# A two-layer hybrid trunk on one core: Toeplitz tiles in partition groups, score matmuls side by side, stick-breaking attention by pairs of heads

## The chip, the core and the metric

One NeuronCore of a Trainium2 chip runs the whole kernel. The metric is the device time of one execution in microseconds (us); the kernel before has 1127.8 as the median of three runs (1125.94 to 1127.84). One further execution was profiled.

## What is computed

Two layers over 256 tokens of width 1024, all in fp32. The parts that the change touches, cut from the reference:

```python
# stick-breaking attention: 8 heads of 64, strictly causal
z = einsum('bhqd,bhkd->bhqk', q, k) * 64 ** -0.5
log_1mb = where(mask, log_sigmoid(-z), 0)
later = cumsum(log_1mb, axis=3, reverse=True) - log_1mb
w = where(mask, exp(log_sigmoid(z) + later), 0);  y = w @ v
# differential attention: 4 heads, two 64-wide score components each
p1 = softmax(mask(q1 @ k1.T)); p2 = softmax(mask(q2 @ k2.T)); o = (p1 - lam * p2) @ v
# S5 state-space branch: 32 groups of 16 channels, 64 complex states
x_t = lam_bar * x_(t-1) + b_bar @ u_t;  y_t = Re(c @ x_t) + d * u_t
```

Around these stand RMSNorms, one wide input projection, gated merging, cross-attention and a squared-ReLU MLP, all as large matrix products.

## The kernel before

**Units.** A layer's weights are walked in units (`plan`), two chunks of 128x1024 each, by SyncE's DMA into a ring `raw`. ScalarE (ACT, `fn`, L897) rounds a chunk to fp32r, the rounded format, as `w_hi`; VectorE (DVE, `tt`, L1311) makes the remainder `w_lo` (`prep`, two units ahead, L917 and L1316); TensorE (PE) does three products hi*hi, hi*lo, lo*hi (`three`, L1788). "T" units have 256-column matmuls (48) or "N" units 512-column ones (24). Units 0 to 13 are u, sq, sk, sv, dq, dk, dv (two each), 14 to 25 the gates, 26 and 27 glu; up and down units of the MLP come last.

**Sides.** `side_stages` (L127) hangs small stages behind units, sorted by `RANK` (L232) for units 7 to 26. PE runs a unit, then its side. VectorE's loop (L1723) is: evacuate the unit's banks, `stage` of each side stage, `prep`, then `later` of each. ScalarE's (L1190) is the same with `prep` ahead of the stages up to unit 15. Each engine keeps its order; semaphores count bank fills (`full`) and releases (`free`), and `before` makes a matmul wait for the last user of its bank. There are eight PSUM banks: A0 to A3, T0, T1 (units), X0, X1 (stages).

**Stick-breaking**, head h: behind unit 6+h `sb_s` (L1972) puts scores into X0 as 256 and 128 columns (the causal triangle, keys on the partitions), VectorE masks them into z (L1606), then in `later` ScalarE takes |z|, exp, ln (L1157) and VectorE adds max(z, 0) (L1684) to give nl = -log(1-beta). Behind unit 7+h `sb_u` (L1983) multiplies nl by a triangle `tri` and by `ones` into X1, in fp32, to get the cumulative sums; VectorE subtracts, ScalarE exponentiates. Behind 8+h `sb_p` (L1992) multiplies with the values into 64 partitions of A3; after two heads the bank is split into hi and lo. z and nl are double-buffered.

**Differential**, j = 0 to 7 (two query tiles by four heads): behind 16+j `da_s` (L2006) makes two components into X0 and X1, 128 columns (j < 4) or 256; behind 17+j `da_t` (L2015) transposes the weights into X1, copied out by ScalarE (L1113); behind 18+j `da_p` multiplies by the values. `RANK` puts da_t ahead of the next da_s.

**Toeplitz tables.** `p_k` (L1902) makes for each of 16 pairs of groups a 32x128 tile (4 fp32 matmuls of 32 stationary columns, L1911, and a 32x32 diagonal, L1913), four tiles to a bank, n = 0 to 3; ScalarE copies them into `kt` (L997), 4 copies for each n, shifted to 4 places. Layer 0's set lies behind units 5 and 6 in A0 and A1, layer 1's behind two down units of layer 0's MLP in X0 and X1. Next come `p_bt` transposes in the same banks, copied by ScalarE. Four `ssm_in` stages stand behind units 9 to 12 (VectorE in `later`, L1449, signal `s_ready`) and four `ssm_out` behind 11 to 14. ScalarE's evacuation of dv (unit 13) waits for all four `s_ready` (L1037).

GpSimd builds constants and the tables of powers and phases.

## Time and profile before

| | us |
|---|---|
| median of three runs | 1127.8 |
| the profiled execution, its own time | 1125.67 |
| its span | 1124.0 |
| PE busy | 1075.9 (96%) |
| DVE busy | 738.7 (66%) |
| ACT busy | 581.3 (52%) |
| POOL (GpSimd) busy | 170.2 (15%) |

Busy is the time in which at least one instruction of the engine ran, as a share of the span. A fp32 matmul stands as two rows, one for each pass; its end is modelled, so neighbouring matmuls overlap in the rows, and the time from start to start is the better measure. Shapes are written rows*columns of the stationary side, then output partitions x columns.

### The profile page before, as it was taken

To read this page: it belongs to the slowest core of one execution; us is meant where nothing else is said; L and a number is where in the kernel's file an instruction comes from. 1 tells how busy PE (TensorE), PEld (TensorE's weight loads), DVE (VectorE), ACT (ScalarE), POOL (GpSimd) and SP (SyncE) were. 2 spreads that over 40 slices of the span, in tenths; PEclk is the share of its full clock that TensorE was granted. 3 is DMA by queue.
4 is the path that set the end of the run, shared out by engine and by line. 5 is a ranking of instruction groups with operands and counts; after the bars stand their busy time and mean duration, and the time that the engine had idled before them with its cause. 6 is when DMAs were issued, how large, how long until landed. Compare 5 with 4: busy or idle time off the path is not lost. (4 is left out here: it accounts for less than half of the span.)

```text
span 1124.0 us, 18664 instructions
## 1 busy us (share of the span) xinstructions
PE 1075.9 (96%) x7186; PEld 967.0 (86%) x7186; DVE 738.7 (66%) x1071; ACT 581.3 (52%) x907; POOL 170.2 (15%) x305
## 2 busy tenths in 40 slices
PE   4989999999999899999989999999999999999996
PEld 4967889989998799987979878998998979989995
DVE  5864965778876565795465468477787647555554
ACT  7445445546665555544654444544555556444442
POOL 5992100000000003996000001000000000000000
PEclk9999999999999999999999999999999999999998
DMA  8723235446554296553556532364465535666662
GB/s 226 209 73 113 89 100 155 147 142 209 175 166 139 88 255 189 178 179 107 161 183 189 167 108 90 95 193 138 151 223 156 161 117 169 187 188 188 188 187 76
DMA packets 148988, 175.62 MB, mean 156 GB/s; under 512 B 26658, under 2 KB 106660, under 8 KB 148900
## 3 DMA queue, kind: packets, MB, share of 16 engines
q1 hardware_dynamic: 148484, 174.16, 51.4%
q8 instruction: 58, 0.95, 0.3%
q10 hardware_dynamic: 416, 0.26, 0.2%
q14 instruction: 30, 0.25, 0.1%
HBM read 171.25 MB, written 3.15 MB: 155 GB/s over the span
## 5 line engine op out<-in xcount | busy, mean ns | idle before, releaser
L1311 DVE TENSOR_TENSOR s_w_lo<-s_raw,s_w_hi 128x1024 fp32r<-128x1024 f32 x312 | 377.5, 1239 | 138.9 <-ACT s_w_hi L897 135.4
L897 ACT ACTIVATE s_w_hi<-s_raw 128x1024 fp32r<-128x1024 f32 x312 | 321.4, 1055 | 202.4 <-PE p_T L1791 137.6
L1789 PE MATMUL p_T<-s_hT_hi,s_w_hi 128*128 128x256 f32 x1152 | 330.6, 287 | 7.5 <-DVE s_hT_lo L1380 5.8
L1790 PE MATMUL p_T<-s_hT_lo,s_w_hi 128*128 128x256 f32 x1152 | 326.8, 284 | 0.0
L1791 PE MATMUL p_T<-s_hT_hi,s_w_lo 128*128 128x256 f32 x1152 | 326.7, 284 | 0.0
L1789 PEld LDWEIGHTS p_T<-s_hT_hi,s_w_hi 128*128 128x128 f32 x1152 | 221.8, 192 | 12.8 <-issue 11.4
L1790 PEld LDWEIGHTS p_T<-s_hT_lo,s_w_hi 128*128 128x128 f32 x1152 | 222.0, 193 | 0.4
L1791 PEld LDWEIGHTS p_T<-s_hT_hi,s_w_lo 128*128 128x128 f32 x1152 | 221.8, 193 | 0.0
L1789 PE MATMUL p_A<-s_w_hi,s_bT_hi 128*128 128x512 f32 x320 | 125.3, 392 | 2.4 <-DVE s_bT_lo L1311 2.4
L1790 PE MATMUL p_A<-s_w_lo,s_bT_hi 128*128 128x512 f32 x320 | 124.7, 390 | 0.0
L1791 PE MATMUL p_A<-s_w_hi,s_bT_lo 128*128 128x512 f32 x320 | 124.6, 389 | 0.0
L1789 PEld LDWEIGHTS p_A<-s_w_hi,s_bT_hi 128*128 128x128 f32 x320 | 60.2, 188 | 15.1 <-issue 3.2
L1791 PEld LDWEIGHTS p_A<-s_w_hi,s_bT_lo 128*128 128x128 f32 x320 | 60.1, 188 | 12.7
L1790 PEld LDWEIGHTS p_A<-s_w_lo,s_bT_hi 128*128 128x128 f32 x320 | 60.1, 188 | 11.7
L725 POOL TENSOR_TENSOR s_small<-s_small 128x16 f32<-128x16 f32 (+1 forms) x130 | 55.8, 453 | 7.0 <-ACT s_small L897 4.7
L1789 PE MATMUL p_T<-s_w_hi,s_hT_hi 128*128 128x512 f32 x128 | 51.9, 406 | 2.4 <-issue 2.4
L897 ACT ACTIVATE s_att<-s_att 128x384 f32<-128x384 f32 (+1 forms) x68 | 36.1, 532 | 32.8 <-DVE s_att L1311 31.0
L1790 PE MATMUL p_T<-s_w_lo,s_hT_hi 128*128 128x512 f32 x128 | 50.6, 396 | 0.0
L1791 PE MATMUL p_T<-s_w_hi,s_hT_lo 128*128 128x512 f32 x128 | 50.6, 396 | 0.0
L897 ACT ACTIVATE s_bT_hi<-s_att 128x512 fp32r<-128x512 f32 x32 | 20.2, 632 | 57.8 <-DVE s_att L1311 57.8
L725 POOL TENSOR_TENSOR s_small<-s_col,s_small 128x16 f32<-128x16 f32 x4 | 1.0, 263 | 310.5 <-ACT s_small L897 310.5
L1789 PE MATMUL p_T<-s_bT_hi,s_w_hi 128*128 128x256 f32 x160 | 45.9, 287 | 0.3 <-issue 0.3
(270 smaller groups left out, 1688.5 us busy)
## 6 DMA issues: line engine op xcount, KB each, us to landing
s_raw<-in_w_in SPq DMA_DIRECT2D x104, 512.0 KB, 3.6
s_raw<-in_w_up SPq DMA_DIRECT2D x64, 512.0 KB, 3.7
s_raw<-in_w_down SPq DMA_DIRECT2D x64, 512.0 KB, 3.8
s_raw<-in_w_branch SPq DMA_DIRECT2D x24, 512.0 KB, 3.9
s_raw<-in_w_out SPq DMA_DIRECT2D x16, 512.0 KB, 4.6
s_raw<-in_w_xkv SPq DMA_DIRECT2D x16, 512.0 KB, 3.7
s_raw<-in_ssm_w_glu SPq DMA_DIRECT2D x8, 512.0 KB, 3.8
s_raw<-in_w_xq SPq DMA_DIRECT2D x8, 512.0 KB, 3.7
```

What stands on the lines that cost most here:

```text
L725: return nc.gpsimd.tensor_tensor(o, i0, i1, op)
L897: return nc.scalar.activation(o, i, f, **kw)
L1311: return V.tensor_tensor(o, i0, i1, op)
L1789: mm(o, lhi, rhi, start=first, stop=False, **kw)
L1790: mm(o, lhi, rlo, start=False, stop=False, **kw)
L1791: return mm(o, llo, rhi, start=False, stop=last, **kw)
```

## The change

The Toeplitz tiles of a table all go into one bank in the first p_k stage: tile 4n+q lies in partitions 32q to 32q+31, columns from 128n, and the four q of a step are issued one after the other; the second p_k stage only copies. Layer 0's table keeps A0, layer 1's X0. Stick-breaking runs by pairs p = 0 to 3: sb_s behind unit 6+2p with the heads' scores in X0 and X1, sb_u behind 7+2p, sb_p behind 8+2p; z and nl hold both heads and have one buffer. nl is split into nl_hi (ScalarE) and nl_lo (VectorE), both fp32r, and the cumulative sums are two fp32r passes of each, with `tri` and `ones` stored as fp32r (built in `att` by GpSimd and copied at the start by VectorE). da_s waits for both banks before its first matmul, and da_t goes to A1.

```diff
-    for h in range(SB_HEADS):
-        after(6 + h, "sb_s", h)
-        after(7 + h, "sb_u", h)
-        after(8 + h, "sb_p", h)
+    for p in range(SB_PAIRS):
+        after(6 + 2 * p, "sb_s", p)
+        after(7 + 2 * p, "sb_u", p)
+        after(8 + 2 * p, "sb_p", p)
...
-        "p_ct": ["X0", "X1"], "sb_s": ["X0"], "sb_u": ["X1"], "turn": ["X0", "X1"],
-        "da_s": ["X0", "X1"], "da_t": ["X1"], "da_o": ["X1"],
+        "p_ct": ["X0", "X1"], "sb_s": ["X0", "X1"], "sb_u": ["X0", "X1"], "sb_p": ["A3"], "turn": ["X0", "X1"],
+        "da_s": ["X0", "X1"], "da_t": ["A1"], "da_o": ["X1"],
...
-        [[["A0", "A1"], ["X0", "X1"]][s[1]][s[2] % 2]] if s[0] in ("p_k", "p_bt") else
+        [[["A0", "A1"], ["X0", "X1"]][s[1]][s[2] % 2]] if s[0] == "p_bt" or s[0] == "p_k" and s[2] == 0 else
...
-        ["A3"] if s[0] == "sb_p" and s[1] % 2 == 0 else
...
+        at = -(-nc.sbuf_base // 32) * 32
...
+        att_r = nc.alloc_sbuf_tensor_at("s_att_r", [P, 2560], F32R, offset=at)
...
-        tri = sb("tri", [P, P])
-        ones = sb("ones", [P, P])
+        tri_r, ones_r = sb("tri", [P, P], F32R), sb("ones", [P, P], F32R)
+        ones = ones_r[:, :].bitcast(F32)
+        tri_0, ones_0 = att[:, 1024:1152], att[:, 1152:1280]
...
-        z_b = [att[:, 768 * i:768 * i + 384] for i in range(2)]
-        nl_b = [att[:, 768 * i + 384:768 * i + 768] for i in range(2)]
+        z, nl = (att[:, 768 * i:768 * i + 768].rearrange("p (h n) -> p h n", h=2) for i in (0, 1))
+        nl_lo, nl_hi = (att_r[:, 768 * i:768 * i + 768].rearrange("p (h n) -> p h n", h=2) for i in (1, 2))
...
-                    b = stage_banks(s)[0]
-                    act.wait_ge(*st.at(*full_at(l, b, s)))
+                    use = ("p_k", t, 0)
+                    b = stage_banks(use)[0]
+                    act.wait_ge(*st.at(*full_at(l, b, use)))
...
-                    for j in range(BL):
-                        rows = slice(32 * j, 32 * j + 32)
-                        ins = fn(kt[rows, 4 * n:4 * n + 4, 32 * j:P], src[0:32, :, 0:P - 32 * j])
-                        ins.then_inc(*st.sig(*freed(l, b, s))) if j == BL - 1 else ins.then_inc(*st.mid())
+                    every = kt[:, :, :].rearrange("p (i q) c -> p q i c", q=4)
+                    for q in (2 * n, 2 * n + 1):
+                        for j in range(BL):
+                            rows = slice(32 * j, 32 * j + 32)
+                            ins = fn(every[rows, q, :, 32 * j:P], src[32 * q:32 * q + 32, :, 0:P - 32 * j])
+                            last = n and q == 3 and j == BL - 1
+                            ins.then_inc(*st.sig(*freed(l, b, use))) if last else ins.then_inc(*st.mid())
...
                     elif kind == "sb_u":
-                        z = z_b[s[1] % 2]
+                        act.wait_ge(*st.at(*freed(l, "X0", s)))
...
-                    elif kind == "sb_p" and s[1] % 2:
+                    elif kind == "sb_p":
...
-                        fn(bT_hi[:, 4 + s[1] // 2, :], bank["A3"][:, 0:T]).then_inc(*st.sig(sb_hi))
+                        fn(bT_hi[:, 4 + s[1], :], bank["A3"][:, 0:T]).then_inc(*st.sig(sb_hi))
...
-                        act.wait_ge(*st.at(*full_at(l, "X1", s)))
+                        act.wait_ge(*st.at(*full_at(l, "A1", s)))
...
-                        fn(pT_b[j % 2][:, 0:nk], bank["X1"][:, 0:nk]).then_inc(*st.sig(*freed(l, "X1", s)))
+                        fn(pT_b[j % 2][:, 0:nk], bank["A1"][:, 0:nk]).then_inc(*st.sig(*freed(l, "A1", s)))
...
-                        z, nl = z_b[s[1] % 2], nl_b[s[1] % 2]
...
+                        act.wait_ge(*st.at(*freed(l, "X1", s)))
                         fn(nl, z, ACT.Abs).then_inc(*st.mid())
...
+                        act.wait_ge(*st.at(nl_made, s[1] + 1))
+                        fn(nl_hi, nl).then_inc(*st.sig(nl_split))
...
+            V.tensor_copy(tri_r[:, :], tri_0).then_inc(*pst.mid())
+            V.tensor_copy(ones_r[:, :], ones_0).then_inc(*pst.mid())
...
-                        h = s[1]
-                        if h >= 2:
-                            dve.wait_ge(*st.at(sbp_done, h - 1))
-                        dve.wait_ge(*st.at(*full_at(l, "X0", s)))
-                        z = z_b[h % 2]
-                        tt(z[:, 0:T], bank["X0"][:, 0:T], mask_s, ALU.min).then_inc(*st.mid())
-                        tt(z[:, T:384], bank["X0"][:, T:384], mask_s[:, 0:P], ALU.min)\
-                            .then_inc(*st.sig(*freed(l, "X0", s)))
+                        p = s[1]
+                        if p:
+                            dve.wait_ge(*st.at(sbp_done, p))
+                        for h, b in enumerate(("X0", "X1")):
+                            dve.wait_ge(*st.at(*full_at(l, b, s)))
+                            tt(z[:, h, 0:T], bank[b][:, 0:T], mask_s, ALU.min).then_inc(*st.mid())
+                            tt(z[:, h, T:384], bank[b][:, T:384], mask_s[:, 0:P], ALU.min)\
+                                .then_inc(*st.sig(*freed(l, b, s)))
...
-                        z = z_b[s[1] % 2]
-                        dve.wait_ge(*st.at(*full_at(l, "X1", s)))
-                        tt(z, z, bank["X1"][:, 0:384], ALU.subtract).then_inc(*st.sig(*freed(l, "X1", s)))
-                    elif kind == "sb_p" and s[1] % 2:
-                        k = s[1] // 2
-                        dve.wait_ge(*st.at(sb_hi, k + 1))
-                        tt(bT_lo[:, 4 + k, :], bank["A3"][:, 0:T], f32(bT_hi[:, 4 + k, :]), ALU.subtract)\
-                            .then_inc(*st.sig(*freed(l, "A3", ("sb_p", s[1] - 1))))
+                        for h, b in enumerate(("X0", "X1")):
+                            dve.wait_ge(*st.at(*full_at(l, b, s)))
+                            tt(z[:, h, :], z[:, h, :], bank[b][:, 0:384], ALU.subtract)\
+                                .then_inc(*st.sig(*freed(l, b, s)))
+                    elif kind == "sb_p":
+                        p = s[1]
+                        dve.wait_ge(*st.at(sb_hi, p + 1))
+                        tt(bT_lo[:, 4 + p, :], bank["A3"][:, 0:T], f32(bT_hi[:, 4 + p, :]), ALU.subtract)\
+                            .then_inc(*st.sig(*freed(l, "A3", s)))
...
-                            dve.wait_ge(*st.at(*full_at(l, "X1", ("da_t", j - 2))))
+                            dve.wait_ge(*st.at(*full_at(l, "A1", ("da_t", j - 2))))
...
-                        z, nl = z_b[s[1] % 2], nl_b[s[1] % 2]
...
-                         .then_inc(*st.sig(nl_ready))
+                         .then_inc(*st.sig(nl_made))
+                        dve.wait_ge(*st.at(nl_split, s[1] + 1))
+                        tt(nl_lo, nl, f32(nl_hi), ALU.subtract).then_inc(*st.sig(nl_ready))
...
-                    elif kind == "p_k":
-                        t, n = s[1:]
+                    elif kind == "p_k" and s[2] == 0:
+                        t, c = s[1], 2 * GC
...
-                        for q in range(4):
-                            i, c = 4 * n + q, 2 * GC
+                        for n in range(4):
...
-                                mm(bank[b][0:c, q * P:q * P + P], bN0[:, r, i, :], ct[:, r, i, :],
-                                   start=(r == 0), stop=False, skip_group_check=True)
-                            ins = mm(bank[b][0:c, q * P:q * P + c], ident[0:c, 0:c], diag_d[:, i, :],
-                                     start=False, stop=True, skip_group_check=True)
+                                for q in range(4):
+                                    mm(bank[b][c * q:c * q + c, n * P:n * P + P], bN0[:, r, 4 * n + q, :],
+                                       ct[:, r, 4 * n + q, :], start=(r == 0), stop=False, skip_group_check=True)
+                            for q in range(4):
+                                ins = mm(bank[b][c * q:c * q + c, n * P:n * P + c], ident[0:c, 0:c],
+                                         diag_d[:, 4 * n + q, :], start=False, stop=True, skip_group_check=True)
...
-                        h = s[1]
-                        r, c = slice(HD * (h % 2), HD * (h % 2) + HD), h // 2
-                        if h == 0:
+                        c = s[1]
+                        if c == 0:
...
-                        mm(bank["X0"][:, 0:T], qk[r, 4 + c, 0:P], qk[r, c, :], start=True, stop=True)
-                        mm(bank["X0"][:, T:T + P], qk[r, 4 + c, P:T], qk[r, c, P:T], start=True, stop=True)\
-                            .then_inc(*st.sig(full["X0"]))
+                        pe.wait_ge(*st.at(*before(l, "X1", s)))
+                        heads = [(b, slice(HD * h, HD * h + HD)) for h, b in enumerate(("X0", "X1"))]
+                        for b, r in heads:
+                            mm(bank[b][:, 0:T], qk[r, 4 + c, 0:P], qk[r, c, :], start=True, stop=True)
+                        for b, r in heads:
+                            mm(bank[b][:, T:T + P], qk[r, 4 + c, P:T], qk[r, c, P:T], start=True, stop=True)\
+                                .then_inc(*st.sig(full[b]))
                     elif kind == "sb_u":
-                        nl = nl_b[s[1] % 2]
                         pe.wait_ge(*st.at(nl_ready, s[1] + 1))
-                        pe.wait_ge(*st.at(*before(l, "X1", s)))
...
-                        o = bank["X1"]
-                        mm(o[:, 0:384], tri[:, :], nl, start=True, stop=True)
-                        mm(o[:, P:T], ones[:, :], nl[:, T:384], start=False, stop=True, skip_group_check=True)\
-                            .then_inc(*st.sig(full["X1"]))
+                        for h, b in enumerate(("X0", "X1")):
+                            pe.wait_ge(*st.at(*before(l, b, s)))
+                            o = bank[b]
+                            mm(o[:, 0:384], tri_r[:, :], nl_hi[:, h, :], start=True, stop=False)
+                            mm(o[:, 0:384], tri_r[:, :], nl_lo[:, h, :], start=False, stop=True)
+                            mm(o[:, P:T], ones_r[:, :], nl_hi[:, h, T:384], start=False, stop=False, skip_group_check=True)
+                            mm(o[:, P:T], ones_r[:, :], nl_lo[:, h, T:384], start=False, stop=True, skip_group_check=True)\
+                                .then_inc(*st.sig(full[b]))
                     elif kind == "sb_p":
-                        h = s[1]
-                        w = z_b[h % 2]
-                        pe.wait_ge(*st.at(w_ready, h + 1))
-                        if h == 0:
+                        p = s[1]
+                        pe.wait_ge(*st.at(w_ready, p + 1))
+                        if p == 0:
...
-                        if h % 2 == 0:
-                            pe.wait_ge(*st.at(*before(l, "A3", s)))
-                        r = slice(HD * (h % 2), HD * (h % 2) + HD)
-                        c = slice(HD * h, HD * h + HD)
-                        mm(bank["A3"][r, 0:T], vN[:, 0, c], w[:, 0:T], start=True, stop=True, skip_group_check=True)
-                        mm(bank["A3"][r, P:T], vN[:, 1, c], w[:, T:384], start=False, stop=True, skip_group_check=True)\
-                            .then_inc(*st.sig(sbp_done))
+                        pe.wait_ge(*st.at(*before(l, "A3", s)))
+                        heads = [(h, slice(HD * h, HD * h + HD), slice(HD * (2 * p + h), HD * (2 * p + h) + HD))
+                                 for h in range(2)]
+                        for h, r, c in heads:
+                            mm(bank["A3"][r, 0:T], vN[:, 0, c], z[:, h, 0:T], start=True, stop=True, skip_group_check=True)
+                        for h, r, c in heads:
+                            ins = mm(bank["A3"][r, P:T], vN[:, 1, c], z[:, h, T:384], start=False, stop=True,
+                                     skip_group_check=True)
+                        ins.then_inc(*st.sig(sbp_done))
                     elif kind == "da_s":
...
+                        pe.wait_ge(*st.at(*before(l, "X0", s)))
+                        pe.wait_ge(*st.at(*before(l, "X1", s)))
...
-                            pe.wait_ge(*st.at(*before(l, b, s)))
...
-                        pe.wait_ge(*st.at(*before(l, "X1", s)))
+                        pe.wait_ge(*st.at(*before(l, "A1", s)))
...
-                            ins = turn(bank["X1"][:, kb * P:kb * P + P], p_b[j % 2][:, 0, kb * P:kb * P + P])
-                        ins.then_inc(*st.sig(full["X1"]))
+                            ins = turn(bank["A1"][:, kb * P:kb * P + P], p_b[j % 2][:, 0, kb * P:kb * P + P])
+                        ins.then_inc(*st.sig(full["A1"]))
...
-                        pe.wait_ge(*st.at(*freed(l, "X1", ("da_t", s[1]))))
+                        pe.wait_ge(*st.at(*freed(l, "A1", ("da_t", s[1]))))
```

Left out are the constants SB_PAIRS = 4, the memsets of tri and ones, signal sizes, ScalarE's bank name for da_t, and waits that name the last p_k or sb_p stage.

## Rows read from the trace of the kernel before

**Rows 1.** The page's head and part 1.
```profile
span 1124.0 us, 18664 instructions
...
PE 1075.9 (96%) x7186; PEld 967.0 (86%) x7186; DVE 738.7 (66%) x1071; ACT 581.3 (52%) x907; POOL 170.2 (15%) x305
```

**Rows 2.** Groups by line; out<-in xcount | busy, mean ns | idle before.
```profile
L1790 PE MATMUL p_T<-s_hT_lo,s_w_hi 128*128 128x256 f32 x1152 | 326.8, 284 | 0.0
...
L1790 PE MATMUL p_A<-s_w_lo,s_bT_hi 128*128 128x512 f32 x320 | 124.7, 390 | 0.0
```

**Rows 3.** Timeline of PE behind unit 9, layer 0: start, us, engine, line.
```profile
107.53 0.65 PE L2003 MATMUL p_A<-s_att,s_vN 128*64 128x256 f32 x2
...
108.33 0.91 PE L1989 MATMUL p_X<-s_att,s_tri 128*128 128x384 f32 x2
...
109.39 0.70 PE L1980 MATMUL p_X<-s_qk 64*128 64x256 f32 x2
...
110.24 2.00 PE L1947 MATMUL p_A<-s_uB,s_bt 128*128 128x63 f32 x16
```

**Rows 4.** Timeline of PE, first two Toeplitz tiles, layer 0.
```profile
57.22 0.62 PE L1911 MATMUL p_A<-s_ct,s_tmp 128*32 128x128 f32 x4
57.77 0.24 PE L1913 MATMUL p_A<-s_att,s_ident 32*32 32x32 f32 x2
57.94 0.62 PE L1911 MATMUL p_A<-s_ct,s_tmp 128*32 128x128 f32 x4
```

**Rows 5.** Timeline of PE, three of the differential score stages, layer 0.
```profile
184.34 0.49 PE L2013 MATMUL p_X<-s_qk 64*128 64x128 f32 x4
...
198.00 1.00 PE L2013 MATMUL p_X<-s_qk 64*128 64x128 f32 x4
...
220.07 1.38 PE L2013 MATMUL p_X<-s_qk 64*128 64x256 f32 x4
```

**Rows 6.** Timeline of VectorE and ScalarE behind unit 6, layer 1.
```profile
633.05 0.62 DVE L1311 TENSOR_TENSOR s_att<-p_X,s_masks 128x256 f32<-128x256 f32 x2 [4.49 <-PE p_X L1981]
...
633.59 2.35 DVE L1311 TENSOR_TENSOR s_w_lo<-s_raw,s_w_hi 128x1024 fp32r<-128x1024 f32 x2
...
633.79 1.64 ACT L897 ACTIVATE s_att<-s_att 128x384 f32<-128x384 f32 x3 [0.54 <-DVE s_att L1311]
...
635.97 0.56 DVE L1684 SCALAR_TENSOR_TENSOR s_att<-s_att 128x384 f32<-128x384 f32 x1
```

**Rows 7.** Groups by line: ScalarE on 1024 columns, VectorE on 768.
```profile
L897 ACT ACTIVATE s_w_hi<-s_raw 128x1024 fp32r<-128x1024 f32 x312 | 321.4, 1055 | 202.4 <-PE p_T L1791 137.6 <-PE p_A L1791 57.9 <-DMA s_raw<-in_w_down 1.7
...
L1311 DVE TENSOR_TENSOR s_qk<-s_vN,s_small 128x768 f32<-128x768 f32 x4 | 3.7, 962 | 0.2
```

**Rows 8.** Timeline around unit 6, layer 0.
```profile
63.92 0.69 DVE L1512 SCALAR_TENSOR_TENSOR s_qk<-p_T,s_r_row 128x512 f32<-128x512 f32 x1
...
64.71 0.55 PE L1789 MATMUL p_T<-s_w_hi,s_hT_hi 128*128 128x512 f32 x1 [1.60 <-issue]
...
75.04 1.77 ACT L897 ACTIVATE s_kt<-p_A 32x512 f32<-32x512 f32 x4 [1.85 <-PE p_A L1913]
```

**Rows 9.** Busy us by stretch; after POOL the granted clock of PE.
```profile
64.96:68.37 3.41, 3.41 (x9) 2.65 (x9) 3.38 (x3) 0.02 (x1) 3.33 (x4) 0.50 0.00 0
81.28:92.66 11.38, 9.75 (x49) 7.46 (x49) 9.06 (x10) 6.74 (x11) 8.22 (x7) 1.00 0.32 94
112.04:122.20 10.16, 10.16 (x54) 8.03 (x54) 9.59 (x18) 4.22 (x6) 0.00 (x0) 1.00 0.32 103
147.88:158.94 11.06, 11.06 (x63) 8.93 (x62) 6.73 (x14) 3.95 (x6) 0.00 (x0) 1.00 0.32 96
```

**Rows 10.** Timeline of VectorE and ScalarE, first state stage and dv, layer 0.
```profile
116.32 0.65 DVE L1311 TENSOR_TENSOR s_gates<-p_A,s_phase 128x504 f32<-128x504 f32 x1
...
121.86 0.56 DVE L1311 TENSOR_TENSOR s_att<-s_att,p_X 128x384 f32<-128x384 f32 x1
...
153.72 1.26 ACT L897 ACTIVATE s_dv<-p_T,s_stat 128x512 f32<-128x512 f32 x2 [7.33 <-PE p_T L1791]
```

26 lines of the change are left out of this document (13 added, 13 removed).

## The prediction

> **What bounds the kernel now.** I read the page first: TensorE (PE) is busy for 96% of the span [rows 1], so time leaves the kernel only where PE work goes away and nothing else takes its place. Next the groups by line: the weight matmuls, which the change leaves alone, differ by 106 ns between 256 and 512 columns, 0.41 ns a column [rows 2]. The small fp32 matmuls cost more per column, and the timeline shows by how much. At the end of a unit one stick-breaking head takes PE from 107.53 to 110.24: weighted values 0.80 us, cumulative sums 1.06, scores of the next head 0.85 [rows 3]. Each fp32 matmul is there as two passes (x2). The Toeplitz tile starts every 0.72 us (57.22, 57.94), of which four 128-column passes and their drain take 0.55 [rows 4]. The differential scores show what lets two matmuls run together: at 184.34 two heads' halves, rows 0 to 63 and 64 to 127 into two banks, are busy for 0.49 us with four passes of 128 columns. At 198.00 the same four take 1.00 (1.38 with 256 columns at 220.07), since the second half waited for the copy out of X1 [rows 5].
>
> **Toeplitz tables, second set** (layer 1's, made in layer 0's MLP). Before: 16 tiles of 0.725 = 11.6 us [rows 4]. After: 4 rounds. In a round four tiles hold four column groups, each with 4 passes. If they overlap as the row groups of [rows 5] do, a round is one tile's passes and drain, 0.55, the small diagonal pair, 0.17, and some stagger, 0.05: 0.77, in all 3.1 us. Saved 8.5. If they don't, the 64 passes stay (0.11 each, 7.0 us) and only 12 of 16 changes of tile shape go: some 8.5 us in all, saved 3.1. I take the first: the rows nearest to it, though they are row groups, show four passes in the time of two. ACT's 16 copies keep their sizes, and PE is waited on by nobody there, so all of it counts.
> Against it, the Trainium skill, TensorE: Matmul & The Clock Gate, Part 3: Packing small matmuls, states that a weight load overlaps a running matmul only when its row group differs; these share their rows. By that rule this term would be 3.1 us, and rival A is the case. The Trainium skill's page TensorEngine Tiling (Array Packing), Key Properties, has tiles load and multiply in parallel; no row here decides between them.
>
> **Toeplitz tables, first set** (layer 0, units 5 and 6): the same 8.5 us on PE, but I book nothing. (a) The first half ended at 62.9 and PE then waited until 64.71 for VectorE's evacuation at 63.92 [rows 8], which doesn't move. (b) Now all tiles lie before unit 6, and p_bt's first bank A0 is free only after ScalarE's last 8 copies. They stand behind the w_hi that waits for unit 6 and ends at 73.19 (75.04 less the idle 1.85), and 8 copies are 2 x 1.77 [rows 8]: 76.7. PE, free at 72.0, waits 4.7. Unit 7 starts at about 78.3, not 81.28 [rows 9]. (c) Then comes the new chain of pair 0, worked out next: 78.2 + 6.9, and some 2.5 to 3 more because GpSimd slows VectorE there (9.06 us busy in unit 7 [rows 9] for what takes 7.3 elsewhere, and twice the columns now): about 88. With both sums, VectorE's two subtractions, the exponential and two bank copies unit 8 starts near 92.7. Before it was 92.66 [rows 9]. Net 0.
>
> **Stick-breaking by pairs.** Before, two heads: 2 x 2.71 = 5.42 us [rows 3]. After: scores of two heads in two row groups 0.86; values in two column groups 0.82 (1.45 without overlap); sums, per head two passes of 384 columns and two of 128. 384 by the line of [rows 2] is 0.17. For 128 columns in the rounded format there is no row: from below 0.06 by the same line, from above 0.22, the cost of the fp32 pair. I take 0.115, near one fp32 pass of 128 columns (four and a drain are 0.55 [rows 4]), because each needs its own weight load. Sums: 2 x (0.34 + 0.23) = 1.14. A pair is 2.82: saved 2.6, over 8 pairs 20.8 us.
>
> **What is added, and who waits.** The chain from scores to sums gets twice as wide and two steps longer. For 384 columns it was: VectorE's minimum 0.62, ScalarE's three functions 1.64, VectorE's 0.56 [rows 6]. For 768: minima 1.25; three functions of 0.85 (1024 columns take 1.055 [rows 7]), 2.6; the add 0.99; then new ScalarE's rounding 0.85 and VectorE's remainder 0.96 [rows 7]; with hand-overs 6.9 us from the last score. PE has one unit, 5.65 us (10.16 from unit to unit [rows 9], less a side of 4.51, 107.53 to 112.04, [rows 3, 9]), and what stands behind the scores in their side. So in layer 1 PE waits at the sums 1.2 us in unit 7 and 0.95 in unit 9; in layer 0 1.0 in unit 9, and in unit 7, where GpSimd's table work slows VectorE, over 2. While ScalarE stands on the add, its evacuation and next w_hi stand behind it; each has a unit to spare.
> From unit 9 to 13 VectorE is the second bound: 9.59 of 10.16 us of a unit [rows 9]. A state-space stage takes it 5.5 us (116.32 to 121.86 [rows 10]; there are four), the weights 2.35 a unit [rows 6]. Its work per pair grows by 0.75 and it stands about 1.2 for ScalarE's rounding. The first state stage starts 4 us earlier (no scores in unit 9), and the four then take 3.6 longer: they end near 152.9. ScalarE's evacuation of dv waits for exactly that in the code; before, it began at 153.72 [rows 10]. Unit 14 needs its first bank, 0.7 later. So unit 14 starts near 153.7 in place of 158.94 [rows 9], though PE could be there 1.4 earlier. Units 14 and 15 give 0.9 each.
> Layer 0, from unit 8: nominal 9.4, less 1.0 and 1.4: 7.0. Layer 1: nominal 10.4, less 1.2, 0.95 and 1.6 for dv: 6.6.
>
> **Differential scores.** Both waits now stand ahead, and the transposed weights go to A1, so X0 and X1 are free when PE comes. The first of eight was paired already; three of 128 columns go from 1.00 to 0.49 and four of 256 from 1.38 to 0.70 (two more passes' worth, 0.21) [rows 5]: 4.2 a layer, 8.4. The last of a layer waited longest, but VectorE is late there and takes that back.
>
> **Edits at nothing.** Two 128-column roundings at the start stand where VectorE waits for positions to land; GpSimd's memsets only change their target; DMAs are the same.
>
> **Sum.** 8.5 + 0 + 7.0 + 6.6 + 8.4 = 30.5 us. The profiled execution took 1125.7 us by its own time (span 1124.0 [rows 1]) and would become 1095.2. It was 2.1 below the median of 1127.8, which becomes **1097**.
>
> **Rivals.**
> A, column groups don't overlap. For: no row shows it, and the four tiles share their rows. Against: row groups do it at once. Tables lose 5.4, values 0.64 a pair where PE is the bound (unit 14 in layer 0 hides most): 1.2 and 2.5. 1097 + 9 = 1106.
> B, the waits at the sums are longer. For: the chain is as long as a unit, and ScalarE may be in an evacuation or w_hi (2.0 us) when the minima come. 2 us more at six of eight pairs, partly absorbed by dv: 1106 to 1109. It needs no fault in the matmul terms.
> C, slower than before: each wait of PE now lets the clock fall. The one fall in the trace followed short Toeplitz work and a 1.6 us wait, and left a granted clock of 0.50 for 3.4 us [rows 9], worth 1.5 us. Its place is the sums' waits: if each of the eight grows by 3 us and brings a fall, 8 x 4.5 = 36 us stand against 30.5, and it ends at 1133. It decides from 30.5 / 8 = 3.8 us a pair. Against: one unit's weights, 5.65 us of dense work, stand between any two waits, and two falls in a row have no row.
> D, better: nl is ready in time, dv doesn't bind: 5 us less, 1092.
> E, the pairs don't overlap even in rows (another order of issue): the scores were in this order once and did. 1104 with overlap elsewhere.
> The first set's wait of 4.7 may bring a fall of its own (+1.5), and the old one may go (-1.5); both are in the range. If 128 columns cost the fp32 price, 8 x 0.42, +3.
>
> **How the numbers follow.** Forecast 0.50, A 0.24, B 0.11, D 0.10, E 0.03, C 0.02. The likeliest is 1097; its own width is 1092 to 1101. The range, 1089 to 1110, takes in A, most of B and D. A measurement of this kernel tells about 0.2% (2.3 us) from no change; every case but C is faster by more. Faster 0.96, same 0.02, slower 0.02.
>
> **What would show it.** Right: Toeplitz rows with starts a few ns apart by fours and some 3 us per table; values of two heads in 0.8 us; a PE gap of about 1 us ahead of the sums in units 7 and 9, ended by VectorE's remainder; unit 8 of layer 0 near 92.7; dv evacuated near 153; differential scores busy for at most 0.7 us. Wrong: 109 ns steps through the Toeplitz rounds (A), gaps over 2 us at the sums (B), granted clock at 1.2 GHz in several stretches (C), a first table that pays on its own.

## The result, and the profile after

The changed kernel takes **1109.7 us** (median of four, 1108.89 to 1111.68) against 1127.8 for the kernel before in the same job: ratio 0.9846, interval 0.9828 to 0.9863. The forecast was 1097. 18 us were gained and not 30.5.

The page's head, part 1 and the clock line of part 2 of the changed kernel; a digit of PEclk stands for 1/40 of the span:

```profile
span 1108.6 us, 18576 instructions
...
PE 1039.0 (94%) x7186; PEld 949.3 (86%) x7186; DVE 745.5 (67%) x1073; ACT 581.8 (52%) x883; POOL 176.7 (16%) x305
...
PEclk9989999999999999999999999999999999999998
```

Against [rows 1], PE is busy for 36.9 us less, and the span is only 15.4 shorter. TensorE's work did go away; some 21 us of it turned into idle time. PE was busy for 96% and is for 94%.

**The matmuls are as forecast.** Timeline of PE and its weight loads (PEld) of the changed kernel: the first two Toeplitz rounds, a pair's values and next scores, and one of the last differential scores.

```profile
57.56 0.38 PEld L1925 LDWEIGHTS p_A<-s_ct,s_tmp 128*32 128x32 f32 x16
57.56 0.64 PE L1925 MATMUL p_A<-s_ct,s_tmp 128*32 128x128 f32 x16
58.13 0.26 PE L1928 MATMUL p_A<-s_att,s_ident 32*32 32x32 f32 x8
58.33 0.64 PE L1925 MATMUL p_A<-s_ct,s_tmp 128*32 128x128 f32 x16
...
100.51 0.65 PE L2019 MATMUL p_A<-s_att,s_vN 128*64 128x256 f32 x4
...
101.31 0.70 PE L1995 MATMUL p_X<-s_qk 64*128 64x256 f32 x4
...
216.83 0.70 PE L2032 MATMUL p_X<-s_qk 64*128 64x256 f32 x4
```

Sixteen passes of four column groups are busy for 0.64 us, where four passes of one took 0.62 in [rows 4]; a round is 0.77 (57.56 to 58.33), as forecast. The values of two heads take 0.80 us for 0.82, their scores 0.86 for 0.86, and differential scores of 256 columns 0.70 where they took 1.38 in [rows 5].

**Where the rest went** is read from stretches between points that both kernels have. The view gives, for each stretch, its length, busy time of PE, PEld, DVE, ACT and POOL, the granted clock as a share of 2.4 GHz, and DMA. The kernel before, from 60 us to unit 8 of layer 0, on to the transposes ahead of the differential part, to the start of layer 1 (which takes in the second table set), to its unit 0 and on to its transposes:

```profile
60.00:92.66 32.66, 28.00 (x159) 20.47 (x159) 21.17 (x21) 16.85 (x31) 28.56 (x40) 0.95 0.23 69
92.66:176.76 84.10, 84.10 (x503) 70.08 (x501) 53.00 (x87) 38.39 (x58) 6.25 (x12) 1.00 0.32 95
176.76:585.36 408.60, 400.96 (x2743) 364.83 (x2742) 279.85 (x388) 224.76 (x355) 84.20 (x130) 1.00 0.55 167
585.36:625.28 39.92, 36.54 (x303) 35.92 (x301) 23.14 (x34) 20.19 (x33) 0.00 (x0) 1.00 0.65 180
625.28:723.55 98.27, 97.44 (x555) 80.29 (x553) 62.67 (x99) 44.59 (x65) 6.23 (x12) 1.00 0.37 110
```

The same stretches of the changed kernel:

```profile
60.00:94.90 34.90, 22.86 (x113) 18.19 (x108) 23.08 (x23) 18.93 (x32) 30.20 (x40) 0.80 0.21 67
94.90:175.12 80.22, 76.29 (x499) 66.61 (x497) 54.68 (x85) 35.85 (x45) 8.43 (x12) 0.98 0.31 99
175.12:574.68 399.56, 388.50 (x2744) 357.27 (x2742) 279.48 (x388) 225.26 (x355) 84.39 (x130) 1.00 0.55 171
574.68:615.18 40.50, 37.54 (x302) 37.23 (x301) 23.32 (x34) 20.42 (x33) 0.00 (x0) 0.96 0.61 178
615.18:710.68 95.50, 89.24 (x555) 76.63 (x553) 66.23 (x100) 44.09 (x53) 8.78 (x12) 0.98 0.36 113
```

Layer 0 from unit 8 gains 3.9 us (84.10 to 80.22; forecast 7.0), the third stretch 9.0 (forecast 4.2 + 8.5), layer 1's last 2.8 (forecast 6.6). Up to unit 8 2.2 are lost where none was expected. Two things are new: PE idles in stretches where it had been busy throughout, and its clock is lower.

**The new waits**, in the view of what PE waited for (in all, times, longest):

```profile
PE p_X L2004 <- DVE s_att_r L1323: 6.4, 5, 1.9
...
PE p_T L1803 <- issue: 5.5, 4, 4.4
PE p_A L1787 <- ACT s_kt L900: 4.9, 1, 4.9
PE p_T L1803 <- ACT s_dv L900: 4.7, 2, 2.4
PE p_A L1787 <- DVE s_att L1710: 3.5, 2, 1.7
```

They are: the sums, for VectorE's remainder; unit 6 ("issue", 4.4, against 1.6 in [rows 8]; VectorE's evacuation for it starts at 64.26, behind table work); p_bt of the first set, for ScalarE's copies; unit 14, for dv; the last differential transposes of each layer, for the weights.

**The clock.** The stretches at half clock (1.2 GHz), in the same columns as above:

```profile
65.36:68.77 3.41, 3.41 (x10) 2.64 (x9) 3.38 (x4) 0.00 (x0) 3.33 (x3) 0.50 0.00 0
75.60:82.42 6.82, 5.12 (x20) 4.13 (x21) 1.47 (x5) 2.88 (x7) 6.51 (x14) 0.50 0.01 2
89.25:92.66 3.41, 3.41 (x15) 3.41 (x16) 1.39 (x3) 2.33 (x4) 2.13 (x3) 0.50 0.26 100
157.52:160.93 3.41, 3.28 (x15) 3.28 (x16) 2.13 (x3) 3.38 (x5) 0.00 (x0) 0.50 0.00 0
577.36:580.77 3.41, 2.86 (x14) 2.89 (x15) 2.97 (x8) 2.53 (x8) 0.00 (x0) 0.50 0.00 0
693.41:696.82 3.41, 3.41 (x18) 3.41 (x18) 2.13 (x3) 3.00 (x4) 0.00 (x0) 0.50 0.00 0
```

Below such a stretch is called a fall. Before there was one (the first of [rows 9]); in either kernel one more begins behind the last matmul and costs none. Each of the six comes during or just behind a wait, but most waits bring none: from 60 us on, 24 steps from one matmul to the next are longer than 1.1 us. Summed over the matmuls in the falls, the steps from start to start are 9.9 us longer than the same steps elsewhere (1.6 before). This is called the excess: what half clock costs if all of it lies on the path.

So there are three accounts of the missing 15 us: the waits alone (rival W below), the waits and the clock behind them (theory G), and matmuls dearer than they look. They need experiments.

### The profile page after: what moved, and what is told of

It is laid out like the page before. It is cut to its first block and busy times, and to the rows that moved or that the text cites. A ratio compares the mean times of both kernels' runs of the same rounds, so it can differ in the third digit from the quotient of the medians.

```text
span 1108.6 us, 18576 instructions
## 1 busy us (share of the span) xinstructions
PE 1039.0 (94%) x7186; PEld 949.3 (86%) x7186; DVE 745.5 (67%) x1073; ACT 581.8 (52%) x883; POOL 176.7 (16%) x305
## 5 line engine op out<-in xcount | busy, mean ns | idle before, releaser
L1803 PEld LDWEIGHTS p_T<-s_hT_hi,s_w_hi 128*128 128x128 f32 x1152 | 223.6, 194 | 17.8 <-issue 11.4
L900 ACT ACTIVATE s_att<-s_att 128x768 f32<-128x768 f32 (+1 forms) x36 | 29.6, 823 | 30.1 <-DVE s_att L1323 29.0
```

The lines of the kernel that those rows point to most:

```text
L900: return nc.scalar.activation(o, i, f, **kw)
L1803: mm(o, lhi, rhi, start=first, stop=False, **kw)
```

## Experiments

Each run was timed in five rounds beside the kernel before on the same chip (medians 1126.2 to 1127.7).

### The parts one by one

**tables_only**: the kernel before, with p_k and its copies as in the change.

> The kernel before with the grouped Toeplitz rounds alone (both table sets), sums and differential scores as before. Theory G (the matmul terms of the prediction were right in size, and part of the gain is given back in new waits of TensorE and in granted-clock falls): the second set gives about 6.6 us (8.5 less a 2.2 us wait for ScalarE's copies), the first set 0 to 1 us (it ends early, waits about 5 us for the copies and runs 6.8 us at half clock): 1127.8 - 7 = about 1121. Rival S (the matmul terms themselves are smaller than forecast, the waits cost nothing): the rounds would take longer than 0.77 us each and the first set would still give something; about 1121 too, but with rounds of over 1 us. Rival F (the forecast's own term): 1119.3.

Measured 1124.0 (1121.0 to 1125.8), ratio 0.9971 (0.9960 to 0.9981): 2.5 us. The rounds take 0.77 us. The long waits stand where the changed kernel has them (4.9 us at unit 6, 5.3 at p_bt), and the profiled run has 10.4 us of excess. Nine runs of one program spread over 4.8 us, with mean clocks of 0.983 to 0.989 that do not sort them. The theory's waits and falls are both there, but it missed by 3 us of time, and by 4.5 of the 7 us of gain that it expected.

**diff_only**: the kernel before, with this alone (left out is the bank's name in the waits and copies of da_t):

```diff
-        "da_s": ["X0", "X1"], "da_t": ["X1"], "da_o": ["X1"],
+        "da_s": ["X0", "X1"], "da_t": ["A1"], "da_o": ["X1"],
...
+                        pe.wait_ge(*st.at(*before(l, "X0", s)))
+                        pe.wait_ge(*st.at(*before(l, "X1", s)))
                         for c, b in enumerate(("X0", "X1")):
-                            pe.wait_ge(*st.at(*before(l, b, s)))
```

> The kernel before with the change of the differential scores alone (both waits ahead, transposed weights into A1). Theory G: each layer gives 4.2 us on the scores and loses about 2 us in a wait ahead of the last transposes, so 2.5 us a layer, 1122.8. Rival F (the forecast's term, with no new wait): 1119.4. Rival I (the 2 us wait of the full change comes from the late stick-breaking work and not from this part): near 1119.4 as well, and no step over 1.5 us ahead of the last transposes.

Measured 1120.3 (1119.8 to 1120.6), ratio 0.9941 (0.9929 to 0.9953): 6.2 us, about 3 a layer, where G had 2.5 a layer. The 2 us step ahead of the last transposes is there in both layers (at 239.41 and 783.12), so I falls: the wait belongs to this part.

**pairs_only**: the kernel before, with the stick-breaking part alone.

> The kernel before with the stick-breaking part of the change alone (pairs of heads, sums in two passes of the rounded format); Toeplitz tiles and differential scores as before. The three parts measured apart: tables alone gave 2.5 us (1126.4 to 1124.0) and differential scores alone 6.2. If they add up, this part is worth 16.7 - 2.5 - 6.2 = 8.0 us against the 20.8 less waits of 5.7 that the prediction booked: 1118.4. Theory G has it between 1117 and 1120, with waits over 1 us ahead of the sums of both first pairs of a layer and 2.6 us ahead of unit 14. Rival X (the parts get in each other's way: the tables' early end brings the wait into unit 7): 1114 or less.

Measured **1127.7** (1120.5 to 1130.2), ratio 0.9995 (0.9976 to 1.0014). A part that takes 20 us of work from TensorE gives no time. Theory G had 1117 to 1120, and missed. Its first wait at the sums is the longest of all, and its falls are long. Timeline of the first sums of layer 0 of this kernel, and windows over four of its falls; the third line is the part of the second fall from the start of unit 14 on:

```profile
91.24 0.69 PE L1999 MATMUL p_X<-s_att_r,s_tri 128*128 128x384 f32 x1 [3.59 <-DVE s_att_r L1318]
```

```profile
90.09:96.92 6.83, 5.08 (x21) 4.71 (x22) 4.43 (x5) 5.19 (x8) 0.25 (x2) 0.50 0.09 36
158.36:165.19 6.83, 5.57 (x26) 5.57 (x27) 3.71 (x5) 4.00 (x5) 0.00 (x0) 0.50 0.00 0
159.62:165.19 5.57, 5.57 (x26) 5.57 (x27) 2.65 (x3) 3.26 (x4) 0.00 (x0) 0.50 0.00 0
...
660.12:666.95 6.83, 6.83 (x24) 5.91 (x23) 6.56 (x11) 1.18 (x2) 3.45 (x4) 0.50 0.01 3
707.90:714.73 6.83, 5.82 (x27) 5.82 (x28) 3.46 (x5) 4.21 (x6) 0.00 (x0) 0.50 0.00 0
```

The excess is some 16 us, over 10 of it in these four. The twelve runs fall into groups by their mean clock: 1120.5 to 1122.4 at 0.990 to 0.992, 1127.7 to 1128.1 at 0.981 to 0.983, 1129.7 to 1130.2 at 0.977 and 0.978. One program, up to 10 us apart, and the clock goes with it. The parts sum to 2.5 + 6.2 - 1.5 = 7 us against 18 together. By the fastest run of each (5.4, 6.7 and 5.7) they sum to 17.8. That would fit parts that add apart from the clock, but the fastest of up to twelve runs is a chosen one, and no run here shows it.

### Is the clock a cause?

**pairs_filled**: pairs_only with idle PE time filled by matmuls of the identity into a free bank.

```diff
+                def fill(b, use, n):
+                    pe.wait_ge(*st.at(*before(l, b, use)))
+                    for _ in range(n):
+                        mm(bank[b][:, 0:P], ident[:, :], ident[:, :], start=True, stop=True, skip_group_check=True)
...
+                    if kind == "sb_u":
+                        fill("X0", s, [14, 4, 0, 0][s[1]] if l == 0 else [5, 7, 0, 0][s[1]])
...
+                    if u == 14:
+                        fill("A3", ("sb_p", 3), 10)
```

> The kernel with the stick-breaking part alone (rounded sums), with identity matmuls in its waits: 14 and 4 ahead of the first two sums of layer 0, 5 and 7 in layer 1, 10 ahead of each unit 14. In its profile 10.4 us of half-clock excess followed these waits. Theory G: those go and the time falls from 1127.7 to 1117 to 1119. Rival W (falls go along with it, but the waits set the time): 1126 to 1128.

Measured **1118.6** (1117.2 to 1120.2), ratio 0.9925 (0.9913 to 0.9937). Work was added, and the median is 9.1 us lower, as G had it; W falls. The fastest runs without fillers (1120.5) come within 2 us of it, at a mean clock of 0.990: the falls vary from run to run, and the fillers make the high clock the rule (0.990 to 0.997). Windows of this kernel, the first at the times of the first fall above, the second as long from the start of unit 14:

```profile
90.09:96.92 6.83, 5.40 (x35) 4.57 (x35) 3.42 (x4) 4.86 (x7) 0.69 (x2) 1.00 0.00 0
156.86:162.43 5.57, 5.57 (x46) 5.57 (x47) 2.65 (x3) 4.33 (x5) 0.00 (x0) 1.00 0.20 65
```

In the first 5.57 us of unit 14, PE has 46 matmul rows where it had 26, at a clock of 1.00 for 0.50.

**filled_waits** is the changed kernel with such fillers.

> The changed kernel with idle TensorE time filled: 128-column matmuls of the identity into a bank that is free, 20 ahead of the first set's p_bt, 4 to 7 ahead of the first two sums of a layer, 10 ahead of unit 14, 12 in the wait of layer 0's MLP norm. Nothing else is touched, and the fillers are a little shorter than the waits. Theory G: the six stretches of half clock (9.9 us in all by the records) fall to the one of the start, so the time goes from 1110 to about 1102. Rival W (only the waits count; work that ran at half clock would have waited later anyway): within 0.2% of the changed kernel, 1108 to 1112, with the clock at full. If the falls stay although the waits are filled: 1110 to 1112, and the clock follows something else than idle time.

Measured 1108.0 (1107.6 to 1108.1), ratio 0.9831 (0.9818 to 0.9843): 1.7 us, at the edge of W's range and not G's 1102. The 12 in layer 0's MLP stood where there was no wait, the fall at 65 us stayed, as did the one at 577, and there was a new one at 519. Up to the transposes of layer 0 it was 3.7 us ahead, for 5.6 of excess that had gone there. This does not decide between G and W.

**all_waits_filled**: fillers also ahead of unit 6, in the second set's p_bt and in layer 1's first transposes.

> The changed kernel with identity matmuls in every long wait of the first table set, the sums, unit 14, the second set's p_bt and the start of layer 1 (17, 20, 7 and 4, 5 and 7, 10 twice, 7, 12 of them, each block a little shorter than its wait); the earlier version of this run had none ahead of unit 6, p_bt of the second set and inside layer 1's first transposes, and spent 12 where there was no wait. Theory G: the waits stay as they are and all falls behind them go (9.9 us by the records of the changed kernel's profile), so about 1109.7 - 8 = 1102, with a narrow scatter. Rival W (clock costs nothing on the path): 1108 to 1110.

Measured 1104.7 (1103.4 to 1106.1), ratio 0.9798 (0.9785 to 0.9811), 5.0 us faster. Windows of this kernel between the same points as above, from its unit 8 (89.77) to the transposes of layer 0, and the last two:

```profile
89.77:168.58 78.81, 77.99 (x526) 68.46 (x525) 56.14 (x86) 35.86 (x45) 13.13 (x17) 1.00 0.33 101
...
568.11:612.05 43.94, 40.62 (x327) 40.21 (x325) 23.25 (x34) 20.30 (x33) 0.00 (x0) 0.96 0.57 164
612.05:706.04 93.99, 92.73 (x599) 80.37 (x597) 66.18 (x100) 44.11 (x53) 8.75 (x12) 1.00 0.39 115
```

Unit 8 comes at 89.77 for 94.90 (5.1 us earlier; the excess that went was 5.5), the stretch to the transposes takes 78.81 for 80.22 (1.4; excess 1.5), and the last stretch 93.99 for 95.50 (1.5; excess 1.4). What fell short of 1102 is the filler at layer 1's start: it lay outside its wait, the fall stayed, and the stretch grew from 40.50 to 43.94. Without those 3.4 us it would be 1101, by estimate.

### What the rounded sums cost

**pairs_fp32_sums**: the changed kernel with fp32 sums.

```diff
-                        act.wait_ge(*st.at(nl_made, s[1] + 1))
-                        fn(nl_hi, nl).then_inc(*st.sig(nl_split))
...
-                         .then_inc(*st.sig(nl_made))
-                        dve.wait_ge(*st.at(nl_split, s[1] + 1))
-                        tt(nl_lo, nl, f32(nl_hi), ALU.subtract).then_inc(*st.sig(nl_ready))
+                         .then_inc(*st.sig(nl_ready))
...
-                            mm(o[:, 0:384], tri_r[:, :], nl_hi[:, h, :], start=True, stop=False)
-                            mm(o[:, 0:384], tri_r[:, :], nl_lo[:, h, :], start=False, stop=True)
-                            mm(o[:, P:T], ones_r[:, :], nl_hi[:, h, T:384], start=False, stop=False, skip_group_check=True)
-                            mm(o[:, P:T], ones_r[:, :], nl_lo[:, h, T:384], start=False, stop=True, skip_group_check=True)\
+                            mm(o[:, 0:384], f32(tri_r[:, :]), nl[:, h, :], start=True, stop=True)
+                            mm(o[:, P:T], ones[:, :], nl[:, h, T:384], start=False, stop=True, skip_group_check=True)\
                                 .then_inc(*st.sig(full[b]))
```

> The changed kernel with the sums of the pairs in fp32 again (one tensor of nl, no rounding by ScalarE and no remainder by VectorE), all else as changed. Theory G: TensorE's sums cost about 0.93 us more a pair, 7.4 in all; the chain is 2.7 us shorter, so the waits ahead of the sums go (2.3, 1.5, 0.7 and 0.4 in layer 0, 1.7, 2.1 and 0.5 in layer 1, less what a step takes without a wait, some 6.5), VectorE is less late at dv (1 to 2 us a layer) and three falls go with them (4.3): about 1103 to 1105. Rival W (no clock term): 1108 to 1109. Rival N (the waits at the sums are nothing, the bound is elsewhere): 1117.

Measured **1099.2** (1097.4 to 1100.3), ratio 0.9753 (0.9740 to 0.9765): 10.5 us faster than the change, and better than G had it. Timeline of PE and ScalarE of this kernel behind unit 13, layer 0:

```profile
147.98 0.81 PE L1999 MATMUL p_X<-s_att,s_tri 128*128 128x384 f32 x2
...
148.84 0.81 PE L1999 MATMUL p_X<-s_att,s_tri 128*128 128x384 f32 x2
...
149.22 1.27 ACT L899 ACTIVATE s_dv<-p_T,s_stat 128x512 f32<-128x512 f32 x2 [6.81 <-DVE s_st_y L1320]
...
149.71 0.56 PE L1971 MATMUL p_A<-s_st_y,s_ct 128*128 128x64 f32 x4
```

The same place in the changed kernel, with VectorE's two steps of the chain:

```profile
148.36 0.96 DVE L1696 SCALAR_TENSOR_TENSOR s_att<-s_att 128x768 f32<-128x768 f32 x1 [0.29 <-ACT s_att L900]
...
150.23 0.96 DVE L1323 TENSOR_TENSOR s_att_r<-s_att,s_att_r 128x768 fp32r<-128x768 f32 x1 [0.91 <-ACT s_att_r L900]
...
151.25 0.44 PE L2004 MATMUL p_X<-s_att_r,s_tri 128*128 128x384 f32 x1
...
152.44 0.61 PE L1976 MATMUL p_A<-s_st_y,s_ct 128*128 128x64 f32 x4
...
156.91 1.27 ACT L900 ACTIVATE s_dv<-p_T,s_stat 128x512 f32<-128x512 f32 x2 [6.71 <-DVE s_st_y L1323]
157.65 0.29 PEld L1803 LDWEIGHTS p_T<-s_hT_hi,s_w_hi 128*128 128x128 f32 x1 [2.51 <-ACT s_dv L900]
```

In fp32 a pair's sums take 1.73 us (147.98 to 149.71), rounded 1.19 (151.25 to 152.44): the format saves 0.54 a pair and not 0.93, 4.3 us in all. For that it makes the chain 1.9 us longer (from the end of the add, 149.32, to the end of the remainder, 151.19), and dv comes at 156.91. In fp32 ScalarE begins with dv at 149.22, ahead of need, and the waits at all sums but the first are gone: the step into them is 0.23 us. The profiled run also has 4.2 us less excess (5.7 for 9.9).

**pairs_fp32_only**: pairs_only with fp32 sums.

> The kernel before with pairs of heads and fp32 sums, Toeplitz tiles and differential scores as before. Rounded, the pairs alone gave 1127.7, no gain. Theory C: with fp32 sums TensorE's work falls by 20.8 - 7.4 = 13.4 us, no new wait at the sums from the second pair on and fewer falls: 1113 to 1116. Rival P (pairing itself is what lets TensorE wait, by tying two heads to one chain): above 1120.

Measured **1111.1** (1109.7 to 1113.1), ratio 0.9856 (0.9843 to 0.9870), 16.6 us faster than pairs_only, and below C's 1113 to 1116; P falls. Pairing is worth 16 us by itself, and the rounded sums take all of it back. The spans of the two profiled runs differ by 18.6 (1128.5 and 1109.9), and the rows come near that: some 13 of excess (16 and 2.9), 6.4 at the sums and 4.7 at dv, less 4.3 of matmul time, make some 20. The excess is the larger half, and pairs_only was profiled in one of its slowest runs.

**split_by_head**: the rounded chain overlapped.

```diff
-                        act.wait_ge(*st.at(nl_made, s[1] + 1))
-                        fn(nl_hi, nl).then_inc(*st.sig(nl_split))
+                        for h in range(2):
+                            act.wait_ge(*st.at(nl_made, 2 * s[1] + h + 1))
+                            fn(nl_hi[:, h, :], nl[:, h, :]).then_inc(*st.sig(nl_split))
...
-                        pe.wait_ge(*st.at(nl_ready, s[1] + 1))
                         for h, b in enumerate(("X0", "X1")):
+                            pe.wait_ge(*st.at(nl_ready, 2 * s[1] + h + 1))
```

(and the same on VectorE).

> The changed kernel with the last three steps of the chain (add, ScalarE's rounding, VectorE's remainder) done per head, so that ScalarE rounds head 0 while VectorE adds head 1, and TensorE's sums of head 0 wait for head 0 alone. The arithmetic and its volume are unchanged, 8 instructions more per layer on ScalarE and 8 more additions and remainders in halves on VectorE. Theory C (the rounded format loses through its chain and the time VectorE stands in it): the chain is 1.0 to 1.3 us shorter, the four waits of 1.1 to 2.3 us shrink by as much, dv comes 2 to 3 us earlier a layer, and one or two falls may go: 1103 to 1106. Rival M (what costs in the rounded format is its matmuls, some 1 us a pair more than the records of the steps say): no more than 1 us gained, 1109.

Measured 1104.9 (1102.6 to 1107.2), ratio 0.9803 (0.9787 to 0.9818): 4.8 us, C holds. In layer 1 the step ahead of the second sums falls from 2.11 to 1.00 us and that ahead of unit 14 from 2.64 to 1.68. Its runs go by the clock too: 1102.6 and 1102.7 at 0.990, 1107.2 at 0.977 to 0.979. The falls did not become fewer in the profiled run, one of the last: it has 17 us of excess.

### The first table set, and versions that beat both

**copies_early**:

```diff
-        pre(0, dict(ct=0, cv=(1, 2), b0=3, bv=(4, 5), k=(5, 6), bt=(6, 7, 7, 8)))
+        pre(0, dict(ct=0, cv=(1, 2), b0=3, bv=(4, 5), k=(5, 5), bt=(6, 7, 7, 8)))
...
-                    k=(up0 + 20, up0 + 21), bt=(up0 + 22, up0 + 23, up0 + 24, up0 + 25)))
+                    k=(up0 + 20, up0 + 21), bt=(up0 + 23, up0 + 24, up0 + 25, up0 + 26)))
```

> The changed kernel with both of ScalarE's table copy stages of the first set placed behind unit 5 (16 copies in a row, ahead of the rounding that waits for unit 6), and p_bt of the second set one unit later each. Theory G: the two waits of TensorE ahead of p_bt (5.3 and 2.2 us) go, and the 6.8 us of half clock at unit 7 with them (2.8 us by the records). Of the first set some 3 to 5 us arrive at unit 8, since pair 0's chain starts earlier but GpSimd's and VectorE's table work stays where it is; of the second all 2: 1109.7 - 6 = about 1104. Rival K (the first set is bound by the table work of VectorE and GpSimd up to unit 8, so the wait only moves): 1107 to 1108.

Measured 1103.5 (1100.2 to 1106.5), ratio 0.9795 (0.9775 to 0.9814): 6.2 us by the medians, with four runs 6 us apart, and K falls. Timeline of ScalarE in the changed kernel:

```profile
60.85 3.58 ACT L900 ACTIVATE s_kt<-p_A 32x512 f32<-32x512 f32 x8 [2.06 <-PE p_A L1928]
69.74 1.06 ACT L900 ACTIVATE s_w_hi<-s_raw 128x1024 fp32r<-128x1024 f32 x1 [5.31 <-PE p_T L1805]
...
73.54 3.61 ACT L900 ACTIVATE s_kt<-p_A 32x512 f32<-32x512 f32 x8
```

and in copies_early:

```profile
61.13 7.21 ACT L900 ACTIVATE s_kt<-p_A 32x512 f32<-32x512 f32 x16 [2.06 <-PE p_A L1928]
```

ScalarE stood idle for 5.3 us with eight copies behind it in its order. They now fill that time, PE comes to the first p_bt of either set without a wait, and the fall at 75.60 is gone. Other falls of its profiled run are longer than in the changed kernel (16 us of excess in all, mean clock 0.978), and it is faster all the same.

**pairs_fp32_copies_early** has both.

> The pairs with fp32 sums, and ScalarE's copies early as in the other run. If the two gains add: 1099.2 - 5 = 1094. If in this kernel the first set's 5.3 us wait is only passed on to the next table wait (the one inside p_bt of units 7 and 8): 1097. Both falls at units 6 and 7 would be down to one.

Measured 1089.7 (1088.7 to 1091.0), ratio 0.9674 (0.9661 to 0.9686): the gains are 10.5, 6.2 and together 20. That is 3 us more than their sum, which intervals of 1 to 2 us on each do not make certain. The profiled run has 4.0 us of excess left.

**by_head_copies_early** is the rounded rival of it.

> The rounded sums with the last three steps of the chain by head, and the copies early. If the gains add (4.8 and 6.2 by the medians): 1098.7. Against pairs with fp32 sums and early copies (1089.7) it shows what the rounded format still costs with its chain shortened. Theory C: its matmuls are 7.4 us cheaper over 8 pairs but dv (1.7 to 2 us a layer) and the falls behind the remaining waits eat more than that: 1095 to 1101. Rival: 1089 or less, the rounded format pays once the chain is overlapped.

Measured 1094.4 (1092.6 to 1097.2), ratio 0.9708 (0.9691 to 0.9724), a little below C's 1095 to 1101. Even overlapped, the rounded sums stay 4.7 us behind fp32.

**fp32_early_filled** fills two waits of the fp32 version.

> Pairs with fp32 sums and early copies, with identity matmuls in its two long waits (19 ahead of unit 6, 12 inside the first transposes of layer 1). Theory G: the 6.8 us of half clock at 62.9 (2.7 us by its records) go, 1.5 to 2.5 us of them on the path: 1087 to 1088. Rival W: 1089.7, the table work of VectorE behind unit 6 sets unit 8 in any case.

Measured 1091.5 (1090.7 to 1092.2), ratio 0.9681 (0.9667 to 0.9694), not faster than without (1089.7) and not G's 1087 to 1088: layer 1's start took 43.9 us for 39.9, the filler outside its wait again. **fp32_early_unit6** has the filler ahead of unit 6 alone.

> Pairs with fp32 sums and early copies, with 19 identity matmuls in the wait ahead of unit 6 alone. Theory G: the 6.8 us of half clock there go (2.7 us by the records) and 1.5 to 2.5 us arrive: 1087.5. Rival V (unit 8 is set by VectorE's and GpSimd's table work, so the time is absorbed in the 2.3 us wait inside p_bt behind unit 7): 1089.7.

Measured 1087.7 (1086.5 to 1089.1), ratio 0.9652 (0.9639 to 0.9665): 2.1 us by the medians, though the intervals just touch. In the profiled runs unit 8 begins at 83.87 for 85.82, so V falls, but new falls at 84.47 and 562.33 take most of it back, and the spans are 1087.3 and 1087.0. That filling here pays shows better in the last run below, against the same kernel without it.

**fp32_early_da_n** moves one stage by one unit:

```diff
-    after(22, "da_n", 0)
+    after(23, "da_n", 0)
```

> Pairs with fp32 sums and early copies, with the normalization of the first half of the differential heads behind unit 23 in place of 22, so that VectorE takes the scores of the last head first. Theory D (the 2 us wait ahead of the last transposes is VectorE's delay by that stage, 2.9 us): the wait goes in both layers, 1.3 to 1.7 us each, 1089.7 - 3 = 1086.7. Rival E (the chain of minima, maximum, exponential and weights is too long for one unit by itself): under 0.5 us gained.

Measured 1086.5 (1085.5 to 1086.7), ratio 0.9639 (0.9626 to 0.9652): 3.2 us, and the wait is gone from both layers; D holds. Timeline of VectorE in the changed kernel shows what stood there:

```profile
233.34 0.69 DVE L1323 TENSOR_TENSOR s_att<-s_att,s_stat 128x512 f32<-128x512 f32 x1
...
234.82 0.76 DVE L1323 TENSOR_TENSOR s_att<-p_X,s_masks 128x256 f32<-128x256 f32 x2 [0.19 <-DVE s_vN L1524]
```

The last head's scores were ready near 232.0 and were taken at 234.82, behind the normalization.

**fp32_early_both** has the last two edits.

> Both of the last two edits. If they add: 1084.5 to 1085. If the fall at unit 6 costs nothing on the path, 1086.7; if neither pays, 1089.7.

Measured **1083.8** (1082.8 to 1084.3), ratio **0.9616** (0.9603 to 0.9629). They add: filling ahead of unit 6 gives 2.7 us here (1086.5 to 1083.8), with no run of either in the range of the other. This version beats the kernel before by 43 us and the change by 26. Page 1 of it: PE is busy for as long as in the changed kernel, in a span 26 us shorter.

```profile
span 1082.5 us, 18637 instructions
...
PE 1036.5 (96%) x7224; PEld 945.8 (87%) x7224; DVE 735.5 (68%) x1065; ACT 575.0 (53%) x875; POOL 178.0 (16%) x305
```

## Why the prediction was wrong

By its own steps:

- **Toeplitz rounds, 8.5 us each.** The matmul term was right to 0.01 us a round. Rival A is out. The Trainium skill's TensorE: Matmul & The Clock Gate, Part 3: Packing small matmuls, lets a weight load overlap a running matmul only when its row group differs. Here the 16 weight loads of a round share their rows and take 0.38 us from 57.56 on, under the 0.64 us of its matmuls, so the measurement goes against that rule, and agrees with the Trainium skill's TensorEngine Tiling (Array Packing), Key Properties. The step that failed is "PE is waited on by nobody there, so all of it counts". Nobody waits for PE, but PE waits at 518.21 for ScalarE's second eight copies, 2.2 us, since p_bt uses the bank that they read. The second set gave 6.6. The first was booked at nothing and lost 2.2: the 5.3 us wait was forecast (4.7), and the 6.8 us of half clock behind it was named as a possible 1.5 and left out of the sum; it has 2.8 us of excess.
- **The pair, 2.82 us.** Values and scores were right; rounded sums 1.19 (forecast 1.14). But the comparison was with [rows 3], where a head's fp32 sums take 1.06: within a pair they take 0.87. So most of "saved 2.6" is due to pairing, and the rounding adds 0.54.
- **The chain and its waits.** Of layer 1, 1.2 and 0.95 us were forecast; PE stood for 1.4 and 1.9 (steps of 1.66 and 2.11, and 0.23 without a wait). The second is the dearer one because something stands ahead of the minima from the second pair on, which the forecast left out: the split of the pair before. In the timeline of the changed kernel ScalarE comes to it only after a rounding (636.80 to 637.86), VectorE's remainder ends near 638.83, and the minima start at 638.86, though the scores were issued by 638.1. "Nominal 9.4, less 1.0 and 1.4" had the waits in the right places and too short: unit 14 came at 157.65 for 153.7, and PE had stood for 2.4 (forecast 1.4) and been late itself.
- **Differential, 4.2 a layer.** The scores gave it. "VectorE late takes that back" was said and not priced: it is 1.7 us a layer, and its cause a stage that could go one unit later.
- **The clock, booked at nothing.** This is the largest step that failed, over half of the missing 15 us. It stood as rival C, sized at 1.5 us a fall, which was right (1.3 to 1.5 us for each 3.4 us at half clock), with "two falls in a row have no row" against it. Six falls came where there had been one, with 8.3 us more excess. all_waits_filled gives 8.0 back where 8.4 of it went, but 5.0 in the medians, since its filler at layer 1's start cost 3.4. C was made to need 3.8 us more wait at each pair before it counted, and so was put at 0.02 as a loss. As a term of the forecast, the excess would have taken 1097 to 1105.

The missing 15 us of the profile by stretch: 2.2 up to unit 8, 3.1 and 3.8 in the two stick-breaking stretches, 1.7 twice for the differential part, 1.9 at the second set, 0.6 at layer 1's start. Rival B's time, 1106 to 1109, came nearest, but by little of its mechanism: it had the waits at the sums 2 us longer at six of eight pairs, and in all they are some 2.6 us longer than forecast (7.8 over 0.23 a step, where the forecast had some 5.2). That the stated range reached up to 1110 is owed to A and B, and neither is what happened.

Open: why a wait brings a fall in one kernel and not in another. The 3.2 us wait at layer 1's start brought one in the changed kernel and none in the kernel before. tables_only stays 3 us above what its theory gave, with falls as a possible cause; it wasn't run with its waits filled. Why the same program has more falls in one run than in another is open too.

## What to carry to other kernels

In a kernel whose TensorE is busy throughout, price a new wait as the wait and, at the upper bound, a stretch at half clock behind it (1.3 to 3.2 us here, behind six of 24 long steps), and compare runs of one kernel by their mean granted clock before believing a difference of a few us. Take time from the waiting side first: a copy or a normalization that stands one unit too early or too late in an engine's order cost 3 to 6 us here, and was moved by changing a unit number. A cheaper matmul format that needs two more steps on other engines is worth only what is left of it when the chain is on the path.
